# Attention: rotary scores in two rounded passes, and VectorE's order of maximum and scaling

## The reference, cut to what matters

```python
s = (jnp.einsum('bqhd,bkhd->bhqk', q_nope, k_nope)
     + jnp.einsum('bqhr,bkr->bhqk', q_rope, k_rope)).astype(jnp.float32) * MLA_SCALE
p = jax.nn.softmax(s, axis=-1).astype(v.dtype)
o = jnp.einsum('bhqk,bkhd->bqhd', p, v)
return o.reshape(b, -1, MLA_H * D_V) @ w_o
```

## Time and profile before

| | us |
|---|---|
| median of 3 runs | 3535.21 (3531.07 to 3535.79) |
| span of the profiled execution (its own time is not given apart from it) | 3531.6 |
| TensorE busy | 3277.4 (93%) |
| VectorE busy | 1808.9 (51%) |
| ScalarE busy | 1262.9 (36%) |
| GpSimd busy | 1563.3 (44%) |
| mean granted TensorE clock | 0.975 |

### The profile page before, as it was taken

One profiled execution on the slowest core, in us unless ns is written; L12 is line 12 of the kernel. 1 busy time (PEld: TensorE's weight loads), 2 busy tenths in 40 slices (PEclk: granted clock), 3 DMA queues, 4 the chain that ended last, 5 costly groups with the idle time before them and its releaser, 6 DMA issues.

```text
span 3531.6 us, 75186 instructions
## 1 busy us (share of the span) xinstructions
PE 3277.4 (93%) x29474; PEld 3040.5 (86%) x29474; DVE 1808.9 (51%) x3093; ACT 1262.9 (36%) x2095; POOL 1563.3 (44%) x1041
## 2 busy tenths in 40 slices
PE   5899999999999998898688899999998999999998
PEld 2689999899899997796577788999997867899997
DVE  7743765564526555859834443447545643521113
ACT  3343223422532224546422334432234133532223
POOL 0355333554553334435577744643344301563334
PEclk9999999999999999999799999999998999999999
DMA  7544554433445443436734433445443201342223
GB/s 274 168 119 144 207 184 155 123 118 101 120 141 203 150 143 111 128 113 218 238 105 113 119 77 120 132 149 193 158 137 96 81 1 33 117 143 73 76 72 121
DMA packets 208667, 465.51 MB, mean 132 GB/s; under 512 B 88928, under 2 KB 98720, under 8 KB 207904
## 3 DMA queue, kind: packets, MB, share of 16 engines
q1 hardware_dynamic: 179904, 442.50, 39.8%
q10 hardware_dynamic: 28512, 19.45, 1.7%
HBM read 420.82 MB, written 41.06 MB: 131 GB/s over the span
## 4 chain that ended last, share of the span: by engine, by line
issue 65%; POOL 17%; POOLq 8%; PE 4%; DVE 3%; DVEq 1%; ACT 0%; DMA 0%; ACTq 0%; SPq 0%
POOL ws L757 17%; POOLq L797 3%; POOLq L794 3%; PE banks L886 1%; PE banks L865 1%; PE banks L870 1%; PE banks L896 1%; POOLq L765 1%; PE banks L1165 0%; DVE bt L2934 0%; POOLq L803 0%; DVEq L2964 0%; DVEq L2924 0%; DVE ar L2953 0%; DVEq L2935 0%
## 5 line engine op out<-in xcount | busy, mean ns | idle before, releaser
L757 POOL TENSOR_TENSOR ws<-wr,ws 128x1024 fp32r<-128x1024 f32 x509 | 1239.5, 2436 | 1827.4 <-ACT ws L1743 1826.5
L1743 ACT ACTIVATE ws<-wr 128x1024 fp32r<-128x1024 f32 x509 | 537.8, 1057 | 1036.9 <-PE banks L870 442.0
L865 PE MATMUL banks<-hs,ws 128*128 128x320 f32 x3712 | 564.8, 309 | 0.5 <-DVE acc L2775 0.3
L865 PEld LDWEIGHTS banks<-hs,ws 128*128 128x128 f32 x3712 | 549.1, 188 | 1.6 <-DVE hs L2877 0.7
L886 PE MATMUL banks<-hs,ws 128*128 128x320 f32 (+2 forms) x2624 | 442.6, 319 | 39.1 <-DVE hs L2515 14.4
L886 PEld LDWEIGHTS banks<-hs,ws 128*128 128x128 f32 x2624 | 401.4, 192 | 66.5 <-issue 23.7
L886 PE MATMUL banks<-fs,ws 128*128 128x320 f32 x2304 | 374.1, 312 | 13.2 <-DVE fs L3255 7.1
L2656 DVE SCALAR_TENSOR_TENSOR mjunk<-mr,banks 128x1024 f32<-128x1024 f32 x284 | 335.6, 1219 | 71.8 <-DMA mr<-in_m_slabs 48.3
L886 PEld LDWEIGHTS banks<-fs,ws 128*128 128x128 f32 x2304 | 344.1, 188 | 31.5 <-issue 12.8
L865 PE MATMUL banks<-fs,ws 128*128 128x320 f32 x2048 | 310.8, 309 | 0.0
L865 PEld LDWEIGHTS banks<-fs,ws 128*128 128x128 f32 x2048 | 303.0, 188 | 0.0
(11 more groups left out here) (325 smaller groups left out, 4003.0 us busy)
## 6 DMA issues: line engine op xcount, KB each, us to landing
wr<-in_w_slabs SPq DMA_DIRECT2D x509, 512.0 KB, 3.6
mr<-in_m_slabs SPq DMA_DIRECT2D x167, 512.0 KB, 5.1
ar_d<-ar SPq DMA_DIRECT2D x16, 640.0 KB, 3.3
bk_d<-bt SPq DMA_DIRECT2D x16, 640.0 KB, 6.0
bk<-bk_d SPq DMA_DIRECT2D x16, 640.0 KB, 5.3
ar<-ar_d SPq DMA_DIRECT2D x32, 320.0 KB, 6.1
mx<-in_m_slabs SPq DMA_DIRECT2D x16, 512.0 KB, 6.7
rkv_d<-relu ACTq DMA_DIRECT2D x16, 320.0 KB, 4.0
```

Of the source, the lines that this page charges most:

```text
L757: pool.tensor_tensor(ws[s % 2][:, 1, :], wr[:, s % 2, :], ws[s % 2][:, 0, :].bitcast(F32), ALU.subtract).then_inc(lo_ready, 1)
L865: pe.matmul(pu[:, t % 2, h, 0:HT], ws[s % 2][:, 0, k * P:(k + 1) * P], src[:, k, part, h * HT:(h + 1) * HT], start=(k + part == 0), stop=F ...
L1743: act.activation(ws[s % 2][:, 0, :], wr[:, s % 2, :], ACT.Copy).then_inc(hi_ready, 1)
```

## The change

The past keys move to the front of `kn` and `kr`, so a latent group has two pieces of 320 keys. The rotary queries are rounded by ScalarE into free rows of `hs` and the rest is subtracted by VectorE; the rounded part of a head stays on its own 64 partitions and the rest is brought by DMA to the other 64 (`stacked(h)`). Since both halves of `kr` hold the same key, one rounded matmul over 128 partitions makes (high + low query) x high key, and a second over 64 partitions makes high query x low key. On VectorE `maximum(n + 1)` and `normalise(n)` change places.

```diff
-KEYS = (((0, HT, 0, 0), (HT, LAT, 1, 0), (T, TK, 1, LAT - HT)), ((LAT, T, 0, 0),))
+KEYS = (((0, HT, 0), (HT, T, 1)), ((T, TK, 0),))
+STACK = ((0, 0), (1, 0), (2, 0), (5, 1), (6, 1), (5, 0), (6, 0), (7, 0))
...
+        def stacked(h):
+
+            return hs[:, STACK[h][0], STACK[h][1], :]
...
-                        sp.dma_start(kr[64 * h:64 * h + 64, T:TK], a["krc"]).then_inc(mla_landed, 16)
+                        sp.dma_start(kr[64 * h:64 * h + 64, 0:PAST], a["krc"]).then_inc(mla_landed, 16)
...
-                pe.wait_ge(rope_done, 5)
+                pe.wait_ge(q_stacked, 16 * MH)
+                pe.wait_ge(k_split, 1)
                 pe.wait_ge(kc_read, 2)
...
-                    for c, (p, e, b, o) in enumerate(KEYS[q == 4]):
-                        out = pu[:, n % 2, b, o:o + e - p]
-                        pe.matmul(out, acc[:, h, q * P:(q + 1) * P], kn[:, h, p:e], start=(o == 0), stop=False,
-                                  skip_group_check=True)
-                    for c, (p, e, b, o) in enumerate(KEYS[q == 4]):
-                        out = pu[:, n % 2, b, o:o + e - p]
-                        mm = pe.matmul(out, qr[r:r + 64, h // 2, q * P:(q + 1) * P], kr[r:r + 64, p:e],
-                                       start=False, stop=True, skip_group_check=True)
+                    turns = slice(q * P, (q + 1) * P)
+                    for p, e, b in KEYS[q == 4]:
+                        pe.matmul(pu[:, n % 2, b, 0:e - p], acc[:, h, turns], kn[:, h, p:e], start=True, stop=False)
+                    for p, e, b in KEYS[q == 4]:
+                        pe.matmul(pu[:, n % 2, b, 0:e - p], stacked(h)[:, turns], kr_high[:, p:e], start=False, stop=False)
+                    for p, e, b in KEYS[q == 4]:
+                        mm = pe.matmul(pu[:, n % 2, b, 0:e - p], stacked(h)[r:r + 64, turns], kr_low[r:r + 64, p:e],
+                                       start=False, stop=True)
...
-                    for i, kt in enumerate((0, 1, 2, 3, 5)):
+                    for i, kt in enumerate((5, 0, 1, 2, 3)):
...
+                def query_highs(i0, i1):
+
+                    for i in range(i0, i1):
+                        act.wait_ge(rope_done, i + 2)
+                        act.activation(stacked(2 * i)[0:64, :], qr[0:64, i, :], ACT.Copy).then_inc(q_rounded, 1)
+                        act.activation(stacked(2 * i + 1)[64:128, :], qr[64:128, i, :], ACT.Copy).then_inc(q_rounded, 1)
...
+                    if j == 14:
+                        query_highs(0, 2)
+                    if j == 15:
+                        query_highs(2, 4)
+                        act.wait_ge(mla_landed, 16 * 6)
+                        act.activation(kr_high[:, :], kr[:, :], ACT.Copy).then_inc(k_rounded, 1)
                 slab[0], tile[0] = s0 + 16, used[15]
+                for i in range(MH // 2):
+                    act.wait_ge(q_split, 2 * i + 2)
+                    act.dma_start(stacked(2 * i)[64:128, :].bitcast(F32), qr_low[0:64, i, :].bitcast(F32)).then_inc(q_stacked, 16)
+                    act.dma_start(stacked(2 * i + 1)[0:64, :].bitcast(F32), qr_low[64:128, i, :].bitcast(F32)).then_inc(q_stacked, 16)
...
+                def query_low(h):
+
+                    r = slice(64 * (h % 2), 64 * (h % 2) + 64)
+                    dve.wait_ge(q_rounded, h + 1)
+                    dve.tensor_tensor(qr_low[r, h // 2, :], qr[r, h // 2, :], stacked(h)[r, :].bitcast(F32), ALU.subtract
+                                      ).then_inc(q_split, 1)
+
+                n = 0
                 for b in range(2):
                     for kt in range(TK // P):
                         take_tile(vk[:, kt, b * 512:(b + 1) * 512], False)
+                        if n < MH:
+                            query_low(n)
+                        if n == MH:
+                            dve.wait_ge(k_rounded, 1)
+                            dve.tensor_tensor(kr_low[:, :], kr[:, :], kr_high[:, :].bitcast(F32), ALU.subtract
+                                              ).then_inc(k_split, 1)
+                        n += 1
...
                 for n in range(n_items):
-                    normalise(n)
                     if n + 1 < n_items:
                         maximum(n + 1)
+                    normalise(n)
```

More of the change, by code:

```diff
@@ L161, in build @@
         kn = place("kn", [P, MH, TK])
+        qr_at = cursor[0]
         qr = place("qr", [P, MH // 2, T])
+        qr_low = place("qr_low", [P, MH // 2, T], F32R, at=qr_at)
+        kr_at = cursor[0]
         kr = place("kr", [P, TK])
+        kr_low = place("kr_low", [P, TK], F32R, at=kr_at)
         kvs = place("kvs", [P, KVR // P, 2, PAST], F32R)
@@ L174, in build @@
         sin = place("sin", [P, LAT], at=relu_at + 4 * LAT)
+        kr_high = place("kr_high", [P, TK], F32R, at=relu_at)
         smax = place("smax", [P, 2, 2], at=relu_at + 8 * LAT)
@@ L394, in build @@
         rope_done = sem("rope_done")
+        q_rounded = sem("q_rounded")
+        q_split = sem("q_split")
+        q_stacked = sem("q_stacked")
+        k_rounded = sem("k_rounded")
+        k_split = sem("k_split")
         cache_split = sem("cache_split")
@@ L1616, in latent_attention @@
                 pe.wait_ge(mla_landed, 16 * 6)
-                swapped(0, kr[:, 0:LAT], t_kr)
+                swapped(0, kr[:, PAST:PAST + LAT], t_kr)
                 pe.wait_ge(h_ready, h_tiles[0] + 2 * (NQ + NKV))
@@ L3171, in take @@
                     c = slice(h * HT, (h + 1) * HT)
-                    to = latent(j, h) if j < NQ + NKV else kr[:, c]
+                    to = latent(j, h) if j < NQ + NKV else kr[:, PAST + h * HT:PAST + (h + 1) * HT]
                     dve.tensor_copy(to, pu[:, t % 2, h, 0:HT]).then_inc(tile_read, 1)
@@ L3179, in latent_attention @@
                 dve.tensor_copy(ckvo[:, :, :], lkv[:, :, LAT:T])
-                dve.tensor_copy(kro[:, :], kr[:, LAT:T]).then_inc(ckv_ready, 1)
+                dve.tensor_copy(kro[:, :], kr[:, PAST + LAT:TK]).then_inc(ckv_ready, 1)
                 for h in range(2, MH):
@@ L3190, in latent_attention @@
                                           ).then_inc(cache_split, 1)
-                rotate(0, kr[:, 0:LAT])
+                rotate(0, kr[:, PAST:PAST + LAT])
                 for b in range(2):
                     dve.wait_ge(kc_done, b + 1)
-                    dve.tensor_copy(kn[:, 4 * b:4 * b + 4, T:TK], pm[:, :].rearrange("p (h n) -> p h n", h=4)
+                    dve.tensor_copy(kn[:, 4 * b:4 * b + 4, 0:PAST], pm[:, :].rearrange("p (h n) -> p h n", h=4)
                                     ).then_inc(kc_read, 1)
                     for j in range(4):
-                        take_tile(kn[:, 4 * b + j, 0:T])
+                        take_tile(kn[:, 4 * b + j, PAST:TK])
                         if j % 2:
```

## The result

The changed kernel takes 3602.6 us (median of 4 runs, 3599.7 to 3616.3) against 3535.5 for the kernel before in the same session; the ratio is 1.0194, 95% interval 1.018 to 1.0208. It is slower by 67 us, where 71 were forecast. The profiled execution is the longest of the four, 3616.3 us with a span of 3614.3; the other three took 12 to 17 us less. Its mean granted clock is 0.959, that of the other three 0.965 or 0.966, so more time at the low clock is the likely cause of its extra 13 us over the median, but no trace of the other three shows where they saved it.

A forecast was written before the change was run, and what follows sets the result against it. The kernel was taken as one chain on TensorE: 3531.6 us span + 24.3 (scores -25.8, idle +53.4, today's low spell -3.3) + 3 operands + 46 clock + 1 = 3606 us. Forecast's own range 3580 to 3640, whole range 3556 to 3650.

The forecast's parts named there:

- VectorE's order: Attention stage, last layer: transposes wait behind the next group's maximum, 2.0 us per latent turn; idle time +53.4 us.
- Saving of the scores: Attention stage: rounded rotary scores and two key pieces cut latent-group scores from 2.45 to 1.72 us; -25.8 us altogether.
- Operands: Value tiles ahead of the stage: VectorE's subtractions delay them, one possibly meeting GpSimd's split; +3 us, bounds 0 and +8.
- Clock: Attention stage: gaps bring TensorE's granted clock down at the first or second gap of most heads; +46 us.
- the 40%: Share of the stage's 116 us of TensorE work taken to run at the low clock, giving +46 us.
- Interpolation by mean clock: Stage's clock read from stretches with known busy share: 0.65 busy lies at 0.81, worth 27 us.
- The 17 gaps with 10 falls behind them: Earlier trace: of 17 TensorE gaps of 1.75 to 2.12 us begun at full clock, 10 preceded low level within 5 us.
- The clock holds: Rival for the attention stage: the gaps leave TensorE's clock at full speed, 3560 us; chance 0.20.
- Dear passes: Rival for the rotary scores: rounded passes cost as much as fp32, about 3640 us; chance 0.06.
- Low throughout: Rival for the attention stage: the clock stays low throughout, value products included, 3676 us; chance 0.13.
- faster: Rival for the turns: TensorE or VectorE reaches over program order and covers the wait, 3510 us; chance 0.05.
- the signs named ahead: Steady-state marks: periods 4.3 and 6.3 us, waits 2.0, scores 1.72, first scores about 2825, stage clock 0.7 to 0.85.

The follow-up runs named there:

- the order alone: Kernel before, fp32 scores kept, with only VectorE's loop changed to maximum of n+1, then scaling of n: 3626.4 us, ratio 1.0249.
- old order: Changed kernel with VectorE's loop put back to scaling of group n, then maximum of n+1: 3530.2 us, ratio 0.9978.
- two ahead: Changed kernel, VectorE's new order kept, with TensorE issuing scores two groups ahead of the transposes: 3518.0 us, ratio 0.9939.
- full rows: Changed kernel with scores two groups ahead and the second rounded pass over 128 partitions instead of 64: 3512.5 us, again 3513.6 us.
- the filled kernels: Changed kernel with twelve or six unread rounded matmuls before transposes of turns without value products ahead: 3572.5 and 3573.5 us.
- the half-filled kernel: Changed kernel with six unread rounded matmuls between scores and transposes of turns without value products ahead: 3573.5 us, ratio 1.0099.

## Why the prediction held, step by step

Time 3606 forecast, 3602.6 measured. The mechanism is the forecast one, a wait in every turn and the low clock that comes with it. That the number came out within 4 us is partly luck: one term failed its bounds and others made up for it.

- **VectorE's order: right.** Forecast +53.4 us of idle TensorE, measured 58.7 - 9.5 = +49.2. A wait is 1.85 us, not 2.0: the reciprocal starts 0.07 behind the negation, and the transposes 0.61 behind the scaling instead of 0.70. The 0.70 of the earlier trace rows was no latency of the scaling alone, since TensorE was busy with scores until then. The fourth turn of a head was hidden as said, and in head 0, without value products, 1.31 us were paid for 1.4. The experiment with the order alone shows the same 57 us of waits.
- **Saving of the scores: mis-sized, and outside its bounds.** Forecast -25.8 (bounds -22 to -29). TensorE's busy time at full clock in the stage is 145.9 less 3.3 of low spell = 142.6 before, and 126.8 and 125.7 in the two changed kernels whose clock held (old order, two ahead), 126.2 in the mean: -16.4. (The kernel before with scores two ahead, all at full clock, has 143.9; by it the saving is 17.6.) The failed step is "the 64-row pass is priced like the 128-row one: today's 64-row scores are no faster than the 128-row ones". No faster was right, but the earlier trace rows have them 0.10 us slower already (1.28 against 1.18), and a rounded pair of 64 rows behind one of 128 costs 0.28 us more than a 128-row pair does. So 2.45 us became 1.95, where 1.72 were forecast; with full rows scores take 1.67. The context group saved 0.10 instead of 0.3 (0.73 to 0.63 us in the changed kernel with the old order), another 1.6 us.
- **Operands: +3 forecast, +4.5 measured** (tiles 19.5 to 24.0). Of this 3.4 to 3.5 are at full clock: in four changed kernels whose clock was 1.00 over the tiles they took 22.9 to 23.0 us. The other 1.1 is a low spell, with a clock of 0.93 over the stretch, which the forecast had no term for. One subtraction met the weight split and lost more than the 1.4 allowed for it:

```profile
2816.39 2.38 POOL L772 TENSOR_TENSOR ws<-wr,ws 128x1024 fp32r<-128x1024 f32 x1 [8.63 <-ACT ws L1759]
2816.50 2.96 DVE L3240 TENSOR_TENSOR qr_low<-qr,hs 64x640 fp32r<-64x640 f32 x1
```

  It started 0.11 us behind the split and ended 0.69 behind its end; the others take 0.82, so it stood for 2.14 us, and TensorE's next tile waited 2.06. The Trainium skill, page "SBUF — State Buffer", section "SBUF: two separate sides", says that VectorE with two memory inputs and a GpSimd operation that reads memory lock each other out for a whole instruction; the trace agrees with these 2.14 us. No wait for the stacking DMAs shows.
- **Clock: right in kind; its size fits the profiled execution and is too large for the median.** +46 forecast on a work of 116 us. Busy time in the stage is 172.3 against those 126.2 at full clock, 46.1 us, and the filled kernels bring back 43 to 45 of it. In the median they bring back 33 to 38. The size is a matter of luck: the 40% was a choice between 0 and 116, and 37% of a larger work came out in the slowest of four executions. The pattern was not as forecast either. The clock did not fall once a head and stay low until the value products; it rose again between turns, and gaps of 1.58, 1.85 and 1.85 us passed at 1.00 (the row 2972 to 2988 above). Interpolation by mean clock (27 us) was too low, the bound far too high. The 17 gaps with 10 falls behind them depend on the way of counting, in windows of half a microsecond: by the starts and modelled ends of TensorE's instructions the same trace has 11 idle gaps of 1.75 to 2.12 us that began at full clock, 9 of them followed by the low level within 5 us, and the last of the 17, in the window 3042 to 3048 of the earlier trace rows, has no single gap longer than 1.43 us.
- **The sum of the stage:** -16.4 + 49.2 + 46.1 - 3.3 = 75.6, measured 75.7; the terms are busy and idle time, so they add up by construction. The rest of the span's growth of 82.7 us is the tiles, 4.5, and 1.8 ahead of them and 0.8 behind the stage, less than the scatter there.
- **What cancelled in the median.** Missing saving +9.4, shorter waits -4.2, operands +1.5, and the kernel before itself 3 us above the 3532.6 that the sum starts from: together 10 us more than forecast. The measured median is 3 us less than forecast, so some 13 us of the low clock's 46 are not there in it. This is an estimate by subtraction from these runs, and it agrees with the 33 to 38 us of the filled kernels.
- **Rivals.** "The clock holds" (3560) is what the half-filled kernel shows, at 1.0099 or about 3570. "Dear passes" had a grain of truth in the 64-row pass. "Low throughout" and "faster" did not happen; the latter's condition, a wait under 0.8 us, is not met. Of the signs named ahead, the periods were 4.47 and 6.67 us (4.3 and 6.3), the first scores stood at 2828.35 (2825) and the stage's clock was 0.76 (0.7 to 0.85).

## What to carry to other kernels

When two engines hand groups to each other, write out which of the engine's own instructions the consumer stands behind. Moving an operation ahead of another on an in-order engine pays only if its input is ready then; a maximum over scores that the other engine makes last turns a hidden chain into a wait per group. Running the producer one group further ahead, with the same two score buffers, made the same order the better one. Where a gap can't be removed, it can pay to shorten it: unread work that filled more than half of each wait made this kernel some 35 us faster.

## What the runs showed of the hardware

- Gaps of 1.85 us in a period of 4.47 brought the granted clock of the stage to 0.76, gaps of 0.77 us in the same period, the rest of each wait filled with matmuls, left it at 1.00.
- A rounded pair of 320 columns over 64 rows behind 128-row matmuls takes 0.28 us more than over 128 rows, pass before it included.
- A rounded subtraction of 64 x 640 from memory takes 0.82 us on VectorE and 1.56 to 1.82 on GpSimd; on VectorE it took 2.96 when it started 0.11 us behind a GpSimd split of 2.38 us.
- In profiled executions of the same kernel, with the same instructions, the part ahead of the value tiles took 2800.8 and 2812.2 us.
